# Narrow products in column strips, half modulation blocks between the mLSTM's heads, gate rows in front of the RMS norms

## What is computed

```python
def mlstm_mixer(x, w_in, conv_w, conv_b, i_bias, f_bias, w_out):
    z = x @ w_in
    qk, v, o, i_pre, f_pre = jnp.split(z, [2 * D_MIX, 3 * D_MIX, 4 * D_MIX, 4 * D_MIX + MLSTM_HEADS], axis=-1)
    qk = jax.nn.silu(causal_dwconv(qk, conv_w, conv_b))
    ...
    h = mlstm_chunkwise(q.reshape(shp), k.reshape(shp), v.reshape(shp), i_pre + i_bias, f_pre + f_bias)
    h = h.reshape(B, S, D_MIX) * jax.nn.sigmoid(o)
    return h @ w_out

def hybrid_layer(x, c, ...):
    mod = (jax.nn.silu(c) @ ada_w + ada_b)[:, None, :]
    sh1, sc1, gt1, sh2, sc2, gt2 = jnp.split(mod, 6, axis=-1)
    h = rmsnorm(x, norm1_g) * (1.0 + sc1) + sh1
    ...
    x = x + gt1 * (merged @ w_out)
    h2 = rmsnorm(x, norm2_g) * (1.0 + sc2) + sh2
    x = x + gt2 * hier_moe_2(h2, rg_w, rg_b, re_w, re_b, e_gate, e_up, e_down)
    return x
```

## Time and profile before

| what | value |
|---|---|
| median of 3 runs (lowest to highest) | 2064.83 us (2064.13 to 2068.94) |
| the profiled execution | 2066.57 us, span of it 2064.7 us |
| mean granted TensorE clock | 0.948 of full speed |
| PE, DVE, ACT, POOL busy | 90%, 28%, 16%, 9% of the span |
| chain that ended last | PE 67%, DMA 14%, DVE 12%, issue 3% |
| weights streamed | 432 units, 457.56 MB on the queue |

### The profile page before, as it was taken

The page is one execution under the profiler, slowest core; times in us unless marked ns, Lnnn a source line. Parts: engine busy times, 40 slices in busy tenths (PEclk is TensorE's granted clock), DMA queues, the critical chain, the costliest instruction groups (busy, mean ns, idle before and its releaser), DMA issues.

```text
span 2064.7 us, 21142 instructions
## 1 busy us (share of the span) xinstructions
PE 1850.5 (90%) x6900; PEld 960.8 (47%) x6901; DVE 585.6 (28%) x1284; ACT 335.5 (16%) x608; POOL 187.1 (9%) x329
## 2 busy tenths in 40 slices
PE   7989789898896896999999999999987999888886
PEld 5544323375663332865676558444433333333332
DVE  8584500278534003133156213001022000000002
ACT  1112211111222111003133100102012111011101
POOL 0131122100001121000000000000000111011100
PEclk9887899998897998999999999999998999999999
DMA  8100569937331796342431434333263999999996
GB/s 313 61 1 2 244 228 391 378 144 292 156 123 63 320 380 278 123 163 82 173 133 41 153 153 163 146 140 130 82 263 137 422 422 422 422 422 422 422 422 250
DMA packets 70426, 468.88 MB, mean 227 GB/s; under 512 B 7832, under 2 KB 12096, under 8 KB 15056
## 3 DMA queue, kind: packets, MB, share of 16 engines
q1 hardware_dynamic: 66000, 457.56, 55.0%
q10 hardware_dynamic: 4352, 10.35, 1.5%
HBM read 466.82 MB, written 1.06 MB: 227 GB/s over the span
## 4 chain that ended last, share of the span: by engine, by line
PE 67%; DMA 14%; DVE 12%; issue 3%; ACT 2%; POOL 1%; ACTq 1%; PEldq 0%; SPq 0%; DVEq 0%; PEld 0%; POOLq 0%
PE bank L238 18%; DMA ring_sb<-stream 14%; PE bank L251 12%; PE bank L2433 11%; PE bank L1423 4%; PE bank L2449 4%; PE bank L2473 3%; PE bank L2330 2%; DVE scratch_sb L1163 2%; PE bank L794 1%; PE bank L1698 1%; DVE scratch_sb L1225 1%; PE bank L261 1%; PE bank L2309 1%; DVE scratch_sb L987 1%
## 5 line engine op out<-in xcount | busy, mean ns | idle before, releaser
L2433 PE MATMUL bank<-ring_sb,scratch_sb 128*64 128x512 f32 x1536 | 352.4, 608 | 66.8 <-DMA ring_sb<-stream 28.8
L251 PE MATMUL bank<-xT_sb,ring_sb 128*128 128x256 f32 x1280 | 281.6, 382 | 14.3 <-DMA ring_sb<-stream 14.3
L251 PEld LDWEIGHTS bank<-xT_sb,ring_sb 128*128 128x128 f32 x1280 | 244.8, 192 | 49.9 <-issue 16.4
L2433 PEld LDWEIGHTS bank<-ring_sb,scratch_sb 128*64 128x64 f32 x1536 | 118.5, 139 | 300.6 <-issue 300.5
L238 PE MATMUL bank<-ring_sb,xT_sb 128*128 128x512 f32 x480 | 209.8, 599 | 0.0
L2473 PE MATMUL bank<-ring_sb,scratch_sb 128*64 128x512 f32 x768 | 171.9, 596 | 10.5 <-ACT scratch_sb L2694 10.5
L238 PE MATMUL bank<-ring_sb,scratch_sb 128*128 128x512 f32 x384 | 167.7, 598 | 6.1 <-ACTq L2062 3.6
L238 PEld LDWEIGHTS bank<-ring_sb,xT_sb 128*128 128x128 f32 x480 | 92.1, 192 | 114.2 <-issue 114.1
L2594 DVE TENSOR_TENSOR scratch_sb<-scratch_sb,bank 128x256 f32<-128x256 f32 (+1 forms) x32 | 17.7, 554 | 432.9 <-PE bank L2433 278.0
L238 PEld LDWEIGHTS bank<-ring_sb,scratch_sb 128*128 128x128 f32 x384 | 73.1, 191 | 98.1 <-issue 90.3
L2449 PE MATMUL bank<-scratch_sb 128*128 128x512 f32 x256 | 118.4, 605 | 0.0
(11 more groups left out here) (386 smaller groups left out, 1636.5 us busy)
## 6 DMA issues: line engine op xcount, KB each, us to landing
ring_sb<-stream SPq DMA_DIRECT2D x432, 1024.0 KB, 9.7
rows_sb<-rows ACTq DMA_DIRECT2D x12, 512.0 KB, 4.5
xT_sb<-xT SPq DMA_DIRECT2D x1, 1024.0 KB, 5.7
x_sb<-x SPq DMA_DIRECT2D x1, 1024.0 KB, 18.8
scratch_sb<-bias_by_distance ACTq DMA_DIRECT2D x1, 1024.0 KB, 5.4
out<-x_sb ACTq DMA_DIRECT2D x2, 512.0 KB, 2.6
scratch_sb<-decay ACTq DMA_DIRECT2D x1, 768.0 KB, 5.3
small_sb<-small SPq DMA_DIRECT2D x1, 640.0 KB, 13.4
```

The costliest lines, as they stand in the source:

```text
L251: mm = pe.matmul(t[:, m * SEQ:(m + 1) * SEQ], w[:, k % 4, n0:n0 + P], actT[:, k, :], start=k == 0, stop=k == kt - 1)
L2433: mm = pe.matmul(t[e * TILE:(e + 1) * TILE, :], self.xs[e][:, kk, :], ws[e][:, k, :], start=kk == 0, stop=kk == KT - 1, skip_group_check=True)
```

## The change

1. `small_T` goes. `small_strips` multiplies 32 columns of `small_sb` (the 8 wanted ones first; both gates of the mLSTM lie in one strip) in four column strips, two k tiles each; `keep_strips` copies the bank on ScalarE; a new `small_T` is one product with `fold_sb`, which is now loaded with `small` and `ident`. The sparse attention folds in the product that used to transpose.
2. `fox_u` by halves: four banks, and the four k tiles of xT's first half and of unit 0 for all four, then those of the second. xT is loaded in two halves, the second behind unit 0.
3. In the mLSTM two modulation blocks stand between the key products, two behind the value products, and blocks 4 to 7 in the head loop: Vector weighs half a block behind each scale (`after_scale`), TensorE adds block 4 + g//2 at odd g at the head of `beside`. `finish_mod` stands behind the loop. The stream's order follows.
4. gt1's strips and rows stand in RmsNorm 0, in front of its transposes, and ScalarE copies the rows into `net.rows[:, 1, :]`, from where Merge's Vector takes them; gt1's four units stand in front of the sparse attention's. gt2's strips stand in RmsNorm 1 between the transposes of its two halves of the tokens.
5. In the mixtures TensorE no longer waits for `gathered` ahead of the expert loop; the loop's own wait stays.

```diff
-    def small_T(self, pe, key, name, actT, banks=range(BANKS)):
+    def small_strips(self, pe, key, name, actT, banks=range(BANKS)):
...
+        t = self.T.open(pe, (key, "strips"), banks)
+        for j in range(2):
+            for m in range(4):
+                k = 2 * m + j
+                mm = pe.matmul(t[32 * m:32 * m + 32, 0:SEQ], self.small[:, k, at:at + 32], actT[:, k, :], start=j == 0,
+                               stop=j == 1, skip_group_check=True)
...
+    def small_T(self, pe, key, strips, row, banks=range(BANKS)):
+
         t = self.T.open(pe, key, banks)
-        for k in range(KT):
-            mm = pe.matmul(t[0:n, 0:SEQ], self.small[:, k, at:at + n], actT[:, k, :], start=k == 0, stop=k == KT - 1)
-        self.T.close(key, mm)
+        self.T.close(key, pe.matmul(t[0:8, 0:SEQ], self.fold[:, row:row + 8], strips, start=True, stop=True))
...
-        net.product_T(pe, "fox_u", net.xT, banks=rest)
+        self.first_product(pe, "fox_u", rest)
+        pe.wait_ge(net.sem("small_loaded"), 16 * 3)
+        net.small_strips(pe, "fox_f", "fox_f", net.xT, banks=self.STATE)
         pe.wait_ge(self.s("params_loaded"), 16 * 4)
-        pe.wait_ge(self.s("u_kept"), 2)
+        pe.wait_ge(self.s("u_kept"), 4)
...
+    def first_product(self, pe, key, banks):
...
+        tiles = [net.T.open(pe, (key, j), banks) for j in range(4)]
+        us = []
+        for half in range(2):
+            pe.wait_ge(net.sem(f"xT{half}_loaded"), 16)
+            us.append(net.use_unit(pe))
+            w = us[half][1].rearrange("p (k n) -> p k n", k=4)
+            for j in range(4):
+                for k in range(4):
+                    mm = pe.matmul(tiles[j][:, 0:SEQ], w[:, k, j * P:(j + 1) * P], net.xT[:, 4 * half + k, :],
+                                   start=half == 0 and k == 0, stop=half == 1 and k == 3)
...
             self.pass_mod(b)
-            if b >= 1:
-                self.mod_sum(pe, b - 1)
+            if b >= 2:
+                self.mod_sum(pe, b - 2)
         net.product(pe, ("mlstm_v", 0), net.xT)
         self.pass_mod(4)
+        self.mod_sum(pe, 2)
+        net.product(pe, ("mlstm_v", 1), net.xT)
         self.pass_mod(5)
         self.mod_sum(pe, 3)
-        self.mod_sum(pe, 4)
-        net.product(pe, ("mlstm_v", 1), net.xT)
-        self.pass_mod(6)
-        self.pass_mod(7)
-        for b in range(5, 8):
-            self.mod_sum(pe, b)
...
@@ def beside(self, pe, g):
+        if g == 0:
+            self.pass_mod(6)
+            self.pass_mod(7)
+        if g % 2 == 1:
+            self.mod_sum(pe, 4 + g // 2)
...
+    def after_scale(self, dve, g):
+
+        if g == 0:
+            self.mod_keep(dve, 2)
+            self.mod_keep(dve, 3)
+        self.mod_block(dve, 4 + g // 2, g % 2)
+        if g % 2 == 0 and g:
+            self.mod_keep(dve, 3 + g // 2)
...
@@ RmsNorm.tensor
+        if self.n == 0:
+            gate_strips(net, pe, "gt1", range(BANKS))
+            gate_rows(net, pe, "gt1", self.strips, 0, range(BANKS))
         for i in range(NT):
+            if self.n == 1 and i:
+                gate_strips(net, pe, "gt2", range(BANKS))
...
@@ Merge.tensor
-        gate_strips(net, pe, "gt1", range(BANKS))
...
-        gate_rows(net, pe, "gt1", self.gt, 0, range(BANKS))
...
@@ Mixture.tensor
-        if self.n == 2:
-            gate_strips(net, pe, "gt2", free)
...
-        pe.wait_ge(self.s("gathered"), base("gathered") + KT)
```

## The result

The changed kernel takes 2049.54 us (median of four runs, 2047.68 to 2051.38), the kernel before 2064.48: a ratio of 0.9932, 95% interval 0.9921 to 0.9944. The profiled execution spans 2045.9 us instead of 2064.7.

What follows compares the result with a forecast made beforehand. The prediction took the chain of waits, mostly TensorE, as the bound. Its terms, -8.5 - 3.3 + 25 - 2.5 - 3.9 - 3.1 = +3.7, on 2066.57 us, less 1.7, gave about 2068 us, range 2057 to 2084.

Steps and rivals of the forecast that it cites:

- 3.3: Expert phases: without the wait for gathered tokens, about 1.1 us off at each of three entries, -3.3 us (0 to -6).
- The mLSTM phase: First score 27.7 us earlier, head loop 52.6 us longer because column sums wait for Vector: +25 us (+10 to +40).
- the sum at full clock: mLSTM head loop, first score to output product, added up without slow clock: 97.5 us; 15 for the clock makes 112.5.
- First product: Start of the kernel: product by halves and narrow strips bring the query product forward, -8.5 us (-3 to -9.5).
- Merge: Before Merge's second half: without strips, ScalarE is through with its copies sooner, -3.9 us (-3 to -4.5).
- router: RMS norm 1 and router: strips moved into idle time no longer delay the rank product, -3.1 us (-2 to -4).
- Index product: Sparse attention: the 8-wide product of 6.52 us becomes strips of 1.97, -2.5 us (-1 to -4.5).
- the one-to-one rule: Last expert loop: it takes the same 420.5 us wherever it starts, so shifting its start shifts the end equally.
- B: Rival, mLSTM head loop: TensorE doesn't stand still, loop at Vector's 7.8 us a head; about 2033 us, chance 0.13.
- D: Rival, start: the halves bring unit 0 no sooner, -3 instead of -8.5 us; 2074 us, chance 0.17.
- C: Rival, mLSTM head loop: the clock stays at half throughout, 15 us more; 2083 us, chance 0.20.
- A: The forecast case: sums wait in the mLSTM head loop, clock falls after gaps; 2062 to 2075 us, chance 0.50.

Runs made afterwards that it cites:

- E1: The changed kernel with TensorE's wait for all gathered tokens put back in the three mixtures: 2072.41 us.
- E2: The kernel before with only the wait for gathered tokens taken out of the mixtures: 2036.94 us, ratio 0.9867 to the kernel before.
- E4: The changed kernel with each column sum issued a head later on TensorE, Vector's order as changed: 2016.67 us.
- E5: The changed kernel with eight useless full-size matmuls in front of each of the four column sums in the mLSTM's head loop: 2045.37 us.
- E8: The changed kernel with modulation blocks back in front of the heads and the wait for gathered tokens put back, so only the small edits: 2043.72 us.
- E6: The changed kernel with sums a head later, Vector reading sums 2 and 3 before the first maximum and folding last modulation work behind the gating: 2013.14 us.
- E3: The changed kernel with all modulation blocks back in front of the mLSTM's heads and the stream's order as before: 2019.89 us.

## Why the prediction was wrong

E1 and E2 show that the wait costs this much. Why the branch is long in some turns and short in others they don't show (see the end).

With 21 for 3.3 the forecast would have been 2050. That this lies on the median is in part luck: on the profiled executions the same sum gives 2052.6 against 2047.68, and the 5 us between are other rows of the ledger (-3.5 in Fox's scan part, -1.3 in the mLSTM, -1.1 at the index product, +2.0 ahead of Merge, and smaller ones).

**The mLSTM phase** was right in mechanism and size. First score 28.3 us sooner (27.7), loop 51.9 longer (52.6), by the mechanism given (both places, 487.0 and 598.9, lie some 22 us ahead of the 509 and 621 that were named, since those left out what is won ahead of the phase): TensorE idle before each of the four sums, the half product, turn and score behind them (E4: 33 us for moving the sums, nothing else). The clock within it: taken at 15, shown to be at least 6 and at the sums about 11 (E5); the rest of the 14 us above the sum at full clock lies at the first gap (5.3 us of idle, in E4 followed by 4.94 for a half product) and in score products, which no run separates.

**First product** -8.7 (-8.5), **Merge** -4.0 (-3.9), **router** -2.8 (-3.1): right. **Index product** -3.6 (-2.5): I had held back 1.1 for the clock, which wasn't lost. Between the sparse attention and Merge 2.0 us are lost where nothing was changed; dense products that took 27.7 and 56.9 us take 29.4 and 57.8 there, at a granted clock of 0.94 and 0.95 instead of 1.00 and 0.97, so it is the clock, as in Fox.

**The expert loop of mixture 2 as the end of it all**: the shift of 18.7 at its second turn is the shift of the end, 18.8. From there the one-to-one rule held. From the loop's first product it did not quite: first product to last wait took 418.8 us (1569.44 to 1988.20) instead of 420.5, because the first turn ran at full clock.

**Rivals.** B (TensorE doesn't stand still) and D (halves without effect) didn't happen. C (half clock throughout the loop) neither: 0.74 granted. The time came out below all of A because of a term that all four cases shared; splitting chances over cases does not widen a range for an error that they have in common.

The strips, last: at full clock 16 records of 256 tokens take 1.07 us (changed kernel, 25.57), 0.067 each where a full-width record of the same moving size takes 0.217 (27.82 for 128): 3.2 times. The Trainium skill, "TensorE: Matmul & The Clock Gate", section "Measured speedup vs the span model", has 2.38 times for three column tiles and 3.07 for four row tiles. With four column tiles the measured ratio lies between 3.2 (here, 256) and 3.8 (512 columns), above both.

## What to carry to other kernels

A wait of TensorE is not priced by the idle time behind it alone: ask what its sequencer would otherwise have done ahead of time, which engine waits for a mark that the sequencer sets, and look at the first turns of each loop against the later ones, and at the branch in each. In an in-order queue the place of a small instruction that waits decides over all that stands behind it; moving four sums by one head was worth 33 us, twice the whole change. Take a change of many parts apart before judging it: here one deleted line gives more than the sum, and another part costs 30 us that the total hides.

## What was not expected of the hardware

- A branch of TensorE's sequencer can take 2.25 to 5.34 us instead of 0.2 to 0.4. The line of `pe.If` runs 32 times in each of the ten kernels. It is long 22 times: at the entry of mixture 2 in all ten, in the second turn of mixture 0 in four (all four with a wait for copies), in the second turn of mixture 1 in seven, once at its entry (E5). Each of the 22 overlaps with a transfer of 0.02 MB on an instruction queue, which begins at the latest 3.0 us after the branch and in two cases 0.1 to 0.2 us ahead of it; of the 298 short ones 8 overlap with such a transfer. The view of DMA for 285.75 to 286.00 of the kernel before (queue, kind: packets, MB, share of 16 engines), inside the branch from 283.5 to 288.3:

```profile
q8 instruction: 1, 0.02, 24.9%
```

  That the branch waits for its code is argued from this coincidence, not shown; no run here moves the code.
- What stays open: why the second turn's branch is long. With a wait for all copies it was so in both mixtures (before, E1, E8). Without one it was short in mixture 0 each time, but in mixture 1 short in E2 and E4, 2.25 us in the changed kernel and E6, 5.1 and 5.3 in E3 and E5 (E3 lost 8 us by it against E4, between the router and the third turn). So a head start of a whole copy phase isn't always enough.
- The same code of 100 us took between 102.5 and 107.5 us from kernel to kernel, with the granted clock at 0.75 to 0.80: in a stretch of short bursts a difference of up to 5 us can't be put down to a change.
